# Norms by tokens, head statistics in the state loop, gate rows ahead of keys, sample states in pairs, keys and values split before spreading: an mLSTM and gMLP decoder step on one core

## The reference

```python
def mlstm_chunk_step(carry, inp):                 # the state update
    ...
    s = jnp.einsum('bhld,bhsd->bhls', q, k) * jnp.exp(log_d - m_t[..., None])
    inter = jnp.exp(m_inter - m_t)
    num = jnp.einsum('bhls,bhsv->bhlv', s, v) + inter[..., None] * jnp.einsum('bhld,bhdv->bhlv', q, c_prev)
    ...
    wk = w[..., None] * k
    c_new = decay[..., None, None] * c_prev + jnp.einsum('bhld,bhlv->bhdv', wk, v)
    ...

def mlstm_mixer(x, conv_buf, c0, n0, m0, p, j):
    xm, z = jnp.split(x @ p['mlstm_w_up'][j], 2, axis=-1)
    ...
    h = head_layer_norm(h, p['mlstm_hn_w'][j]).reshape(bsz, s, MLSTM_INNER).astype(x.dtype)
    h = (h + p['mlstm_skip'][j] * xc) * jax.nn.silu(z)
    return h @ p['mlstm_w_down'][j], new_conv, c1, n1, m1

def run_trunk(...):
    for i in range(DEPTH):
        h = rms_norm(x, p['norm_mix'][i])
        ...                                       # mixer
        x = x + out
        h = rms_norm(x, p['norm_ffn'][i])
        x = x + hier_moe(h.reshape(-1, D_MODEL), p, i).reshape(x.shape)
    y = rms_norm(x, p['norm_final'])
```

## Time and profile before

| | us |
|---|---|
| median of 3 runs | 1632.83 |
| lowest, highest | 1629.47, 1633.82 |
| profiled execution, its time | 1633.13 |
| profiled execution, its span | 1631.4 |
| PE busy | 1349.5 (83%) |
| DVE busy | 531.0 (33%) |
| DMA, mean over the span | 327 GB/s |

### The profile page before, as it was taken

One profiled execution on the slowest core, in us unless ns is written; L12 is line 12 of the kernel. 1 busy time (PEld: TensorE's weight loads), 2 busy tenths in 40 slices (PEclk: granted clock), 3 DMA queues, 4 the chain that ended last, 5 costly groups with the idle time before them and its releaser, 6 DMA issues.

```text
span 1631.4 us, 18559 instructions
## 1 busy us (share of the span) xinstructions
PE 1349.5 (83%) x7619; PEld 760.5 (47%) x7622; DVE 531.0 (33%) x1229; ACT 195.1 (12%) x425; POOL 31.8 (2%) x66
## 2 busy tenths in 40 slices
PE   8998999998999856865866899999997666855867
PEld 5654333376764422422432477777543323422424
DVE  5546766735032220220220323640322202211222
ACT  2233223110020000000000111200200000000001
POOL 4000000000000000000000000000000000000000
PEclk8998999998999987988987999999999889888979
DMA  7232999994727999999999974543499999999994
GB/s 208 104 104 63 402 392 392 378 340 171 292 104 311 427 427 429 428 427 429 429 428 429 410 272 140 176 188 128 168 421 429 427 427 428 429 427 429 428 429 194
DMA packets 101341, 532.80 MB, mean 327 GB/s; under 512 B 6410, under 2 KB 24010, under 8 KB 76366
## 3 DMA queue, kind: packets, MB, share of 16 engines
q1 hardware_dynamic: 97472, 526.25, 79.5%
q10 hardware_dynamic: 3360, 5.09, 1.0%
q0 software_dynamic: 448, 0.62, 0.2%
HBM read 492.45 MB, written 39.49 MB: 326 GB/s over the span
## 4 chain that ended last, share of the span: by engine, by line
PE 53%; DMA 28%; DVE 7%; issue 2%; SPq 1%; ACT 1%; DVEq 0%
DMA arena<-in_moe_w_up 28%; PE bank L899 19%; PE bank L1277 10%; PE bank L1299 5%; PE bank L1257 3%; PE bank L1312 3%; PE bank L1030 2%; DVE arena L1662 2%; PE bank L1182 1%; PE bank L1285 1%; PE bank L1191 1%; SPq L390 1%; ACT arena L769 1%; DVE arena L1607 1%; PE bank L993 1%
## 5 line engine op out<-in xcount | busy, mean ns | idle before, releaser
L1277 PE MATMUL bank<-arena,hT 128*32 128x512 f32 x2048 | 263.4, 672 | 197.8 <-DMA arena<-in_moe_w_up 185.6
L899 PE MATMUL bank<-hT,arena 128*128 128x288 f32 x1024 | 260.8, 414 | 3.3 <-DVE hT L1475 3.3
L1277 PEld LDWEIGHTS bank<-arena,hT 128*32 128x32 f32 x2048 | 78.8, 122 | 369.1 <-issue 368.1
L899 PEld LDWEIGHTS bank<-hT,arena 128*128 128x128 f32 x1024 | 195.0, 193 | 62.5 <-ACT arena L574 4.2
L1822 DVE TENSOR_TENSOR arena<-arena,bank 64x512 f32<-64x512 f32 x32 | 22.1, 692 | 531.7 <-ACT arena L769 531.7
L1257 PE MATMUL bank<-arena 128*128 128x128 f32 (+1 forms) x864 | 153.8, 308 | 1.2 <-DVE arena L1797 0.9
L1299 PE MATMUL bank<-arena 128*32 128x512 f32 x1024 | 129.1, 648 | 21.3 <-DVE arena L1826 21.3
L1257 PEld LDWEIGHTS bank<-arena 128*128 128x128 f32 (+1 forms) x864 | 117.3, 187 | 48.7 <-issue 14.4
L899 PE MATMUL bank<-arena 128*128 128x288 f32 x512 | 130.4, 415 | 0.0
L899 PEld LDWEIGHTS bank<-arena 128*128 128x128 f32 x512 | 97.7, 193 | 31.7 <-issue 3.5
L769 ACT ACTIVATE arena<-bank 64x512 f32<-64x512 f32 x32 | 18.8, 588 | 755.3 <-PE bank L1277 755.3
(11 more groups left out here) (352 smaller groups left out, 1027.8 us busy)
## 6 DMA issues: line engine op xcount, KB each, us to landing
arena<-in_moe_w_gate SPq DMA_DIRECT2D x64, 2048.0 KB, 29.8
arena<-in_moe_w_up SPq DMA_DIRECT2D x64, 2048.0 KB, 32.1
arena<-in_moe_w_down SPq DMA_DIRECT2D x64, 2048.0 KB, 25.2
arena<-in_state_mlstm_C SPq DMA_DIRECT2D x32, 1024.0 KB, 8.5
out_C_s<-arena SPq DMA_DIRECT2D x32, 1024.0 KB, 10.5
arena<-in_mlstm_w_up SPq DMA_DIRECT2D x8, 2048.0 KB, 11.4
arena<-in_cmlp_w_in SPq DMA_DIRECT2D x8, 2048.0 KB, 17.1
arena<-in_mlstm_w_down SPq DMA_DIRECT2D x4, 2048.0 KB, 18.0
```

The source lines that it names most:

```text
L899: ins = mm(B[m % 4][:, 0:NT], w[:, k, 128 * i:128 * i + 128], rhs(k), start=(k == 0), stop=(k == kt - 1))
L1277: ins = mm(B[j][CAP * i:CAP * i + CAP, :], xq[h][:, k, CAP * e:CAP * e + CAP], w[i][:, k, :], start=(k == 0), stop=(k == KD - 1), skip_gro ...
```

## The change

- **Start.** The 16 small loads move from ACT to SP, behind the weight vectors and ahead of pages 1 and 2 of the projection. Page 0 comes in two halves with semaphores of their own. The norm is spread behind transposes of tile 6 and not 4. The warm-up has 14 matmuls for 18.
- **Ahead of the loop.** PE transposes the gate rows behind the values and ahead of the keys. Convolution rows and the scores of head 0 come behind the first two spreads. DVE and not ACT copies the convolution rows out. The key scale is folded into the copies of `kT`. Six warm-up matmuls go.
- **Splitting.** DVE splits the 32 sample rows of keys and values into three bfloat16 pieces (`split`, four operations of 32 rows, twice a head). PE spreads them with a bfloat16 matmul of 96 rows (`spread_row`), ACT copies the bank to `wk8` or `v8` (`spread_out`). `parts` with its 12 DVE operations a head is gone.
- **Pairs.** Two requests are done together: eight L1182 matmuls, then updates in the order (i0, b), (i0, b+1), (i1, b), (i1, b+1), `between`, and the other four. The two requests' operands lie in different groups of 32 rows. SP stores both, waits for both, and loads both.
- **Head statistics.** Those of head h - 1 are taken in the loop of head h. The square root stands ahead of z, `ZLAG` is 3.
- **Final norm.** ACT squares the transposed rows out of PSUM with a sum over the row (six operations), so the 16 rows of L828 and the transposes of the norms go.

```diff
-ZLAG = 9
+ZLAG = 3
...
-            load("up", 0, w_up[:, :, 0:512], k8(page("up", 0)))
+            sp.dma_start(k8(page("up", 0))[:, 0:4, :], w_up[:, 0:4, 0:512]).then_inc(s("half_landed"), 16)
+            load("up", 0, w_up[:, 4:8, 0:512], k8(page("up", 0))[:, 4:8, :])
...
-            for q in range(NB * H + 1):
-                if q < NB * H:
-                    sp.wait_ge(s("c_new"), MH * (q + 1))
-                    sp.dma_start(state(O["C_s"], q), cview(q)).then_inc(s(f"c_stored{q % 2}"), 16)
-                if q > 0:
-
-                    r = q - 1
+            for q in range(0, NB * H, 2):
+                for r in (q, q + 1):
+                    sp.wait_ge(s("c_new"), MH * q + 2 * MH - 1 + r % 2)
+                    sp.dma_start(state(O["C_s"], r), cview(r)).then_inc(s(f"c_stored{r % 2}"), 16)
+                for r in (q, q + 1):
                     sp.wait_ge(s(f"c_stored{r % 2}"), 16 * (r // 2 + 1))
                     if r + 6 < NB * H:
                         load_state(r + 6)
...
-            keep_busy(7, 18)
+            keep_busy(7, 14)
...
-                if k == 4:
+                if k == 6:
...
-                for b in range(NB):
-                    q = NB * h + b
-                    pe.wait_ge(s(f"c_landed{q % 6}"), 16 * (q // 6 + 1))
...
+                for pair in range(NB // 2):
+                    two = (2 * pair, 2 * pair + 1)
+                    for b in two:
+                        q = NB * h + b
+                        pe.wait_ge(s(f"c_landed{q % 6}"), 16 * (q // 6 + 1))
+                        for i in range(MH):
+                            mm(B[4][NS * i:NS * i + NS, :], qz[:, i, NS * b:NS * b + NS], cview(q)[:, i, :],
+                               start=(b == 0), stop=(b == NB - 1), skip_group_check=True)
+                    if pair % 2 == 0:
+                        pe.wait_ge(s("spread_out"), 4 * h + 2 + pair)
+                    for half in range(2):
+                        for i in (2 * half, 2 * half + 1):
+                            for b in two:
+                                n = update_number(h, b, i)
+                                g = 32 * (b % 4)
+                                if n >= 4:
+                                    pe.wait_ge(s("c_new"), n - 3)
+                                mm(B[UPD[n % 4]][:, :], wk8[g:g + 32, b // 4, 128 * i:128 * i + 128],
+                                   v8[g:g + 32, b // 4, :], start=True, stop=True).then_inc(s("c_mm"), 1)
+                        between(h, two[half])
...
+            def split(h, a):
+
+                x = (wks[h % 2][0:NS, 2, :], vts[h % 2])[a]
+                if h > 0:
+                    dve.wait_ge(s("spread_mm"), 4 * h)
+                dve.wait_ge(s(("wk", "vtok")[a]), 3 * h + 1)
+                link(copy(pieces[0:32, a, :], x))
+                link(tt(z1[32:64, a, :], x, pieces[0:32, a, :], ALU.subtract))
+                link(copy(pieces[32:64, a, :], z1[32:64, a, :]))
+                tt(pieces[64:96, a, :], z1[32:64, a, :], pieces[32:64, a, :], ALU.subtract).then_inc(s("pieces"), 1)
```

More of the change, by code:

```diff
@@ L585, in _ @@
                 if m < 2:
[L586 removed]
+                    act.activation(kT[:, m, :], B[2 + m % 2][:, 0:NT], ACT.Copy, scale=KSCALE).then_inc(s("q_out"), 1)
             act.wait_ge(s("gate_part"), KI)
@@ L732, in _ @@
                     prompt_state_out(h, 3)
+            act.activation(small[0:1, 60:61], small[0:1, 61:62], ACT.Sqrt)
+            act.wait_ge(s("mv"), 12)
+            act.activation(mvsd, mvsd, ACT.Sqrt, bias=eps5).then_inc(s("hsd"), 1)
+            act.activation(small[0:1, 62:63], small[0:1, 61:62], ACT.Silu)
             for m in range(KI):
@@ L1148, in _ @@
             pe.wait_ge(s("q_out"), KI + 2)
+            pe.wait_ge(s("gates_dve"), 2)
+            pe.wait_ge(s("vtok"), 3)
+            for j, (t0, n) in enumerate(TOK):
+                tr(B[2][0:n, 128 * j:128 * j + 128], rows[:, t0:t0 + n], ident[:])
+            tr(B[3][0:NB, 0:H], catA[0:4, NT:NT + 8], ident[0:4, 0:4]).then_inc(s("gates_pe"), 1)
+            weights(0)
+            for i in range(3):
+                keys_by_token(0, i)
+            pe.wait_ge(s("tm"), 10)
+            pe.wait_ge(s("masks"), 2)
+            spread_row(0, 0)
+            spread_row(0, 1)
             pe.wait_ge(s("cv27"), 2)
```

264 lines of the change are left out of this document (120 added, 144 removed).

## The result

The changed kernel takes 1639.3 us (median, 1638.4 to 1640.3), against 1632.3 us of the kernel before on the same chip. The ratio is 1.0042, with a 95% interval from 1.0027 to 1.0057, so it is slower by 0.4%. The prediction said 1608.8 us and faster. The span of the changed kernel is 1636.6 us against 1631.4. That is 5.2 us more, and the two traces show where they come from.

A forecast was written before the change was run, and what follows sets the result against it. DMA was taken as first bound in the state loop (ceiling about 407 GB/s), engines a close second. Start 4.3, loop 8, z and head norm 10.0 and final norm 2.0 sum to 24.3: 1633.1 - 24.3 = 1608.8 us, range 1600 to 1620.

The forecast's parts named there:

- DMA is continuous from there: State loop's start: with both first states complete at 151.8, DMA runs on unbroken from there, not from the second store.
- The term of + 8 us: State loop: 3.4 us from the earlier start plus 4.6 from fewer waits for `c_new`, together 8, bounds 2 to 10.
- the third rival: State loop: handovers from stores to loads leave DMA dry; at 2.1 us a pair 27 us lost, 1640.7; chance 0.05.
- The shift at the loop's start: State loop's start: continuous DMA begins 6.0 us sooner, less 2.6 for one store more in front, so 3.4 us.
- Start: Kernel start: earlier sample rows 1.5, later norm spread 0.6, half a page 2.2; sum 4.3 us, from 2 to 7.3.
- Ahead of the loop: Before the state loop: first update computed at 144.9, bounds 142 to 148; signs named were update near 140, stores near 148.
- What the loop could give: State loop: at most 6.3 us come back from waits for `c_new`; 4.6 taken, 8 with the shift.
- z and head norm: z to down projection: 12.4 + 2.7 - 3.3 - 1.8 = 10.0 us gained, or 7 if PE's clock falls anyway.
- Final norm: Kernel end: ACT's squares replace L828's 4.05 us on PE; gain between 0 and 4.05, taken as 2.0.
- The bounds: Whole kernel: start 2 to 7.3, loop 2 to 10, z 7 to 10, end 0 to 4.
- That the pairs don't run side by side: Rival, state loop: PE needs 4.3 us a head more of 5.8 slack; time near 1609, counted within the forecast's 0.55.
- That DMA would be faster than 407: Rival, state loop: DMA reaches the 428 GB/s of pure loads and wins 7 us more, 1602; chance 0.11.

The follow-up runs named there:

- before_pair_stores: The kernel before with only SP's state loop changed to pairs: both stores, then wait and load for each; 1652.7 us, ratio 1.0119.
- pairs_single_stores: The changed kernel with SP's old order back (one store, one wait, one load), PE and DVE still in pairs; 1619.8 us, ratio 0.9916.
- no_pairs: The changed kernel with PE, DVE and SP all taking one state at a time, the rest of the change kept; 1616.2 us, ratio 0.9903.
- no_pairs_again: A second run of the changed kernel with PE, DVE and SP at one state at a time, `ZLAG` 3; 1612.1 us, ratio 0.9879.
- pairs_lagged_waits: The changed kernel with each pair's waits and loads moved behind the stores of the next pair; 1640.9 us, ratio 1.0042.
- pairs_pool_loads: The changed kernel with the loads of states moved from SP's stream to POOL's; 1682.1 us, ratio 1.0318.

## Why the prediction was wrong

- **The step that failed** is in the part on the loop: "DMA is continuous from there", with 2 us as the lower bound for pairing that "opens new gaps". SP's order in pairs was taken to cost nothing, and it costs 2.1 us a pair, 27 us over 13 pairs (before_pair_stores has it with PE and DVE untouched, pairs_single_stores is rid of it). The term of + 8 us was - 19.2. All the rest of the miss is small beside these 27 us.
- **The mechanism was in the text**, as the third rival, "The pairs let DMA run dry", with a chance of 0.05. Its price was right: "At 2.1 the loss is 27: 1640.7", against 2.1 us a pair from SP's rows and 1639.3 us. That the total agrees so well is in part luck. The shift at the loop's start was 27.2 - 19.2 = 8.0 us and not 3.4, z gave 6.4 and not 10, and the two misses nearly cancel. And 2.1 was the price of one handover left bare, where the trace has two stretches that add up to it. The rival was dismissed because the second store "covers 2.58 of it if the stores run one behind the other". In four of twelve pairs it does, in four others it does not (193 GB/s in the 2.5 us from 204.85, where at 205 at most 0.3 MB of the store is left). The same doubt already stood in the earlier trace rows: a lone store lands 4.3 to 5.3 us after its issue, so 1.7 to 2.7 of that are no movement, and a cover of 2.58 was never clearly more than the handover's 2.1 to 3.1. Two ranges that overlap are not a chance of 0.05.
- **It also missed the larger part of the loss.** The 6 us behind the handover lose 1.5 us a pair in the mean, the handover itself 0.7. The second part is there in every pair, whether the store covered the handover or not, and its cause is open. Stores in threes are nearly free of it.
- **Start**: 4.3 predicted, 4.6 measured. Right, and the first matmul at 13.88 was expected near 14. The first tile ran at a low clock (the changed kernel's granted clock in 14 to 16 us is 0.69). Its 16 rows took 5.81 us, against 6.91 before and 3.88 at full clock, so the term did not grow to 7.3.
- **Ahead of the loop**: first update at 140.25 (expected 140), first stores at 146.55 (expected 148). Right. With single states on PE and the rest of the change it is sooner still: no_pairs issues its first store at 143.06.
- **What the loop could give**: 4.6 us were expected from fewer waits for `c_new`, 8 with the shift. no_pairs starts z 11.8 and 6.4 us sooner than before in its two profiles (PE's timeline), of which 4.3 and 4.7 come from the start. So 1.7 to 7.5 are there, and without the pairs. That they come from the cheaper spreads is likely, but was not run alone.
- **z and head norm**: 10.0 predicted with bounds 7 to 10, 6.4 measured, below the lower bound. The tail was to be 1.8 and is 3.2. PE's clock fell all the same (0.50 in 412 to 414 us), so 0.8 of the 2.7 came back. z grew by 3.5 (3.3 expected). In no_pairs_again, where the clock stays up, the whole is 5.6 + 2.5 = 8.1.
- **Final norm**: 2.0 predicted, 2.6 measured. Right.
- **The bounds** that "give 1600 to 1622" add up to 1602 at the lower end. It changes nothing.
- **That the pairs don't run side by side** was half right: 0.21 us an update instead of 0.28, not 0.14. It decides nothing, as written.
- **That DMA would be faster than 407**: it is not. The best of the 40 slices end at 409 to 411 in every kernel here.

## What to carry to other kernels

When one queue issues both stores and the loads that refill their buffers, count what is queued at the moment the awaited store lands, and don't count on a transfer's whole size, since part of it may have moved already. SP's order cost 43 us here with no 1 MB store behind the awaited one (1.0266), 19 with one (1.0119) and 3 with two (1.0017). How much one store covered differed from pair to pair. Nor may a load be put behind a wait for the next results (pairs_lagged_waits). The old order, one store, one wait and one load, satisfies both. And where DMA bounds a loop, a faster order on the engines does not shorten it: here the pairs on PE and DVE started z at 321.5 us, single states at 311.5 and 316.9.

## What the hardware showed that I had not expected

- Two 1 MB stores issued 0.5 us apart can move largely together. In the pair at 204.85 us their landings are reported some 2.5 us apart, but soon after the first report at most 0.3 MB are left. In other pairs (231.45, 258.81) DMA moves at 386 to 400 GB/s for 2.5 us from there.
- In the 6 us behind such a handover DMA moves 280 to 349 GB/s at a busy share of 0.91 to 1.01, where 407 come with 1.05.
- From the issue of two loads on an idle queue to most of the full rate it is nearly 3 us (220.22 to 223), with 55 and 193 GB/s in the last two microseconds of it.
- To issue the load of a state takes POOL 0.75 us (pairs_pool_loads) and SP 0.38 (the changed kernel).
- no_pairs has runs from 1604 to 1622 us where the kernel before stays within 1627 to 1638. Its loop ends at 311.5 or 316.9 in two profiles. What varies there was not found.
